# Sample rows of the input projection: four column groups hold quarters of the columns instead of parts of the contraction

## The reference

```python
D_MODEL, SEQ, DEC_BATCH, DEC_SEQ = 1024, 256, 8, 4
xn = rms_norm(x, p['norm_attn_g'])
z = jnp.einsum('btd,de->bte', xn, p['w_in'])
(qa, ck, cv, sk, sv, wk, wv, ng, fq, fk, fv, ff, ga, gb) = jnp.split(z, offs, axis=-1)
```

## Time and profile before

| | |
|---|---|
| median of 3 runs | 924.46 us |
| profiled execution, its own time | 927.73 us |
| its span | 926.0 us |
| TensorE busy | 858.2 us, 93% |
| VectorE busy | 513.4 us, 55% |
| ScalarE busy | 378.6 us, 41% |
| projection stage, first matmul to last ScalarE copy | 17.2 to 110.2 us |

### The profile page before, as it was taken

One profiled execution on the slowest core, in us unless ns is written; L12 is line 12 of the kernel. 1 busy time (PEld: TensorE's weight loads), 2 busy tenths in 40 slices (PEclk: granted clock), 3 DMA queues, 4 the chain that ended last, 5 costly groups with the idle time before them and its releaser, 6 DMA issues. The chain is left out here.

```text
span 926.0 us, 17951 instructions
## 1 busy us (share of the span) xinstructions
PE 858.2 (93%) x7159; PEld 703.4 (76%) x7159; DVE 513.4 (55%) x941; ACT 378.6 (41%) x704; POOL 161.3 (17%) x262
## 2 busy tenths in 40 slices
PE   4999878799999999999998977999979999999997
PEld 3788768689989977655754455997678998989985
DVE  5466567533434566754467434655656565565654
ACT  4346575633334324453224322444243443444432
POOL 2000041311121022333434510000001010110100
PEclk8999989999999899999999999999979999999999
DMA  6442096155424259999999995974054544555412
GB/s 219 150 160 105 10 316 236 60 145 134 165 107 184 92 229 398 346 333 416 406 417 420 388 404 169 297 250 164 10 196 142 162 137 136 177 195 171 136 45 61
DMA packets 90640, 191.89 MB, mean 207 GB/s; under 512 B 7466, under 2 KB 68682, under 8 KB 78186
## 3 DMA queue, kind: packets, MB, share of 16 engines
q0 software_dynamic: 15408, 106.04, 29.4%
q1 hardware_dynamic: 74876, 83.91, 29.0%
q10 hardware_dynamic: 288, 0.97, 0.3%
HBM read 187.44 MB, written 7.64 MB: 211 GB/s over the span
## 5 line engine op out<-in xcount | busy, mean ns | idle before, releaser
L1627 PEld LDWEIGHTS banks<-consts_base,stream_rows 128*128 128x128 f32 x672 | 73.2, 141 | 33.9 <-issue 26.8
L1875 ACT ACTIVATE keys_turned<-banks 128x512 f32<-128x512 f32 x94 | 55.0, 597 | 98.4 <-PE banks L1627 96.2
L258 PE MATMUL banks<-tokens_turned_high,w_gates_high 128*128 128x288 f32 x288 | 86.6, 301 | 3.3 <-PEq L191 2.3
L1627 PE MATMUL banks<-consts_base,stream_rows 128*128 128x128 f32 x672 | 82.7, 276 | 7.4 <-DVE fox_probs_turned L1866 2.6
L259 PE MATMUL banks<-tokens_turned_low,w_gates_high 128*128 128x288 f32 x288 | 85.5, 297 | 0.0
L1166 PE MATMUL banks<-chunks_turned_high,cmp_w_high 64*128 64x256 f32 (+1 forms) x512 | 78.6, 300 | 5.3 <-DVE cmp_w_low L251 2.7
L260 PE MATMUL banks<-tokens_turned_high,w_gates_low 128*128 128x288 f32 x272 | 81.8, 301 | 0.0
L1166 PE MATMUL banks<-chunks_turned_low,cmp_w_high 64*128 64x256 f32 (+1 forms) x512 | 75.4, 287 | 0.0
L1166 PE MATMUL banks<-chunks_turned_high,cmp_w_low 64*128 64x256 f32 (+1 forms) x512 | 75.1, 286 | 0.0
L1856 DVE COPY keys_turned<-banks 128x512 f32<-128x512 f32 x74 | 50.2, 689 | 32.7 <-PE banks L1627 30.2
L251 DVE TENSOR_TENSOR chunks_turned_low<-banks,chunks_turned_high 128x512 fp32r<-128x512 f32 x64 | 41.1, 683 | 46.9 <-ACT chunks_turned_high L246 46.9
(11 more groups left out here) (451 smaller groups left out, 2099.1 us busy)
## 6 DMA issues: line engine op xcount, KB each, us to landing
w_up_gate<-in_w_up SPq DMA_DIRECT2D x12, 1024.0 KB, 7.3
w_up_gate<-in_w_gate SPq DMA_DIRECT2D x12, 1024.0 KB, 9.8
w_down<-in_w_down SPq DMA_DIRECT2D x12, 1024.0 KB, 4.9
w_in_slot<-in_w_in SPq DMA_DIRECT2D x7, 1424.0 KB, 6.0
w_gates<-in_w_in SPq DMA_DIRECT2D x10, 512.0 KB, 6.8
cmp_w<-in_cmp_w_k SPq DMA_DIRECT2D x4, 512.0 KB
cmp_w<-in_cmp_w_v SPq DMA_DIRECT2D x4, 512.0 KB
stream_rows<-in_state_win_k SPq DMA_DIRECT2D x8, 256.0 KB
```

Of the source, the lines that this page charges most:

```text
L258: nc.tensor.matmul(out, lh, rh, start=start, stop=False, **kw)
L1627: ins = nc.tensor.transpose(bank(t)[:, q * P:(q + 1) * P], src, ident)
L1875: copy = lambda a, b: nc.scalar.activation(a, b, ACT.Copy)
```

## The change

`ZQ` = 89 is a quarter of a chunk's columns. Each column group now takes its own quarter of the columns and sums all 8 contraction steps, so the finished sample rows stand in the bank, each quarter at its own partitions. A contraction step is four matmuls of 89 columns with the same stationary rows. The folding product, the buffers `part` and the copy into them go. VectorE copies the four 32 x 89 pieces straight into `z`, at the place where `sample_part` stood. Counts of semaphores are adjusted: `z_out[0]` counts one a chunk, and `sample_out` takes the place of `fold_out`.

```diff
@@ constants
+ZQ = ZC // 4
@@ TensorE, for each chunk
                 if n >= 2:
-                    pe.wait_ge(z_out[0], 2 * n - 2)
+                    pe.wait_ge(z_out[0], n - 1)
                     pe.wait_ge(z_out[1], n - 1)
-                    pe.wait_ge(fold_out, n - 1)
+                    pe.wait_ge(sample_out, n - 1)
...
                 for k in range(KD):
-                    g = k % 4
                     if n == 0 and k % 4 == 0:
                         pe.wait_ge(w_first[k // 4], 16)
-                    m = nc.tensor.matmul(U[3 * u + 2][32 * g:32 * g + 32, 0:ZC], c.xsT[:, k, :], w[u][:, k, :], start=(k < 4), stop=(k >= 4))
+                    for g in range(4):
+                        m = nc.tensor.matmul(U[3 * u + 2][NS * g:NS * g + NS, 0:ZQ], c.xsT[:, k, :], w[u][:, k, g * ZQ:(g + 1) * ZQ],
+                                             start=(k == 0), stop=(k == KD - 1))
                 m.then_inc(z_sums, 1)
...
                 tokens(n, 0)
-                pe.wait_ge(z_out[0], 2 * n + 1)
-                nc.tensor.matmul(U[3 * u + 2][0:NS, 0:ZC], c.k("fold"), part[u], start=True, stop=True).then_inc(folded, 1)
...
@@ VectorE
-            def sample_part(n):
+            def sample_rows(n):
                 dve.wait_ge(z_sums, 3 * n + 1)
-                if n >= 2:
-                    dve.wait_ge(folded, n - 1)
-                nc.vector.tensor_copy(part[n % 2], U[3 * (n % 2) + 2][:, 0:ZC]).then_inc(z_out[0], 1)
+                if n == 0:
+                    dve.wait_ge(zeroed, 1)
+                for g in range(4):
+                    ins = nc.vector.tensor_copy(z[0:NS, 2, at(n) + g * ZQ:at(n) + (g + 1) * ZQ], U[3 * (n % 2) + 2][NS * g:NS * g + NS, 0:ZQ])
+                ins.then_inc(sample_out, 1)
...
-            def sample_rows(n):
-                dve.wait_ge(folded, n + 1)
-                if n == 0:
-                    dve.wait_ge(zeroed, 1)
-                nc.vector.tensor_copy(z[0:NS, 2, cols_of(n)], U[3 * (n % 2) + 2][0:NS, 0:ZC]).then_inc(fold_out, 1)
...
             for n in range(NZC):
-                sample_part(n)
+                sample_rows(n)
...
                 rows0(n)
-                sample_rows(n)
```

More of the change, by code:

```diff
@@ L383, in stage_project @@
         flat = c.h_rows[:, :, :].rearrange("p t d -> p (t d)")
-        part = [flat[:, u * ZC:(u + 1) * ZC] for u in range(2)]
         sq = flat[:, D:D + 3 * FW].rearrange("p (t h e) -> p t h e", t=3, e=HD)
@@ L393, in stage_project @@
         z_out = [c.sem(f"z_copied_{e}") for e in "va"]
-        z_sums, folded, fold_out, zeroed = c.sem("z_sums_ready"), c.sem("z_folded"), c.sem("z_fold_copied"), c.sem("z_sample_zeroed")
+        z_sums, sample_out, zeroed = c.sem("z_sums_ready"), c.sem("z_sample_copied"), c.sem("z_sample_zeroed")
         gains_in, gain_ready, zeros = c.sem("gains_in"), c.sem("q_gains_scaled"), c.sem("q_zeroed")
@@ L446, in turn @@
                 if bank == 0:
-                    pe.wait_ge(z_out[0], 2 * NZC - 2)
+                    pe.wait_ge(z_out[0], NZC - 1)
                 elif number[x] > 2:
@@ L461, in turn_tails @@
                 ins.then_inc(heads_turned, 1)
-                pe.wait_ge(fold_out, NZC - 1)
+                pe.wait_ge(sample_out, NZC - 1)
                 pe.wait_ge(chunks.pe_in, 32)
@@ L469, in turn_nsa_keys @@
                 pe.wait_ge(heads_ready, rank["KK"] + 1)
-                pe.wait_ge(z_out[0], 2 * NZC)
+                pe.wait_ge(z_out[0], NZC)
                 for t in range(3):
                     if t == 2:
-                        pe.wait_ge(fold_out, NZC)
+                        pe.wait_ge(sample_out, NZC)
                     bank = U[3] if t < 2 else U[5]
@@ L551, in square @@
                 n = complete[group]
-                act.wait_ge(z_out[0], 2 * n + 2)
+                act.wait_ge(z_out[0], n + 1)
                 act.wait_ge(z_out[1], n + 1)
-                act.wait_ge(fold_out, n + 1)
+                act.wait_ge(sample_out, n + 1)
                 if rank[group]:
@@ L677, in scale @@
                 dve.wait_ge(roots, rank[group] + 1)
-                dve.wait_ge(z_out[0], 2 * n + 2)
+                dve.wait_ge(z_out[0], n + 1)
                 dve.wait_ge(z_out[1], n + 1)
-                dve.wait_ge(fold_out, n + 1)
+                dve.wait_ge(sample_out, n + 1)
                 lo, heads = rs_at[group], sum(heads for _, heads in groups[group])
@@ L704, in forget_parts @@
                 ff = z[:, :, O_FF:O_FF + NH]
-                dve.wait_ge(z_out[0], 2 * NZC)
+                dve.wait_ge(z_out[0], NZC)
                 dve.wait_ge(z_out[1], NZC)
-                dve.wait_ge(fold_out, NZC)
+                dve.wait_ge(sample_out, NZC)
                 link(nc.vector.tensor_tensor(ff, ff, bcast(c.forget_bias[:, :], 1, 3), ALU.add))
```

## The result

The changed kernel takes 919.65 us (median of 8 runs, 917.43 to 923.14), the kernel before in the same number of runs 925.39 us (921.75 to 929.25). The two medians lie 5.7 us apart. The ratio is 0.9945 with a 95% interval of 0.992 to 0.997, which stands for 5.1 us saved, with an interval of 2.8 to 7.4. The forecast was 921.5 us and 3.0 us saved. Ratios and intervals here leave out one execution, of the run without folds in chunks 2 to 7, which took 1208 us at a mean granted clock of 0.66.

The account below looks back on a forecast made before the run. TensorE, 93% busy, was taken to bound the kernel. Folds -4.9, sample products +0.4 and the clock's fall +1.5 sum to -3.0 us, from the median 924.46 to 921.5 us, range 918.9 to 924.6.

Parts of the forecast that it names:

- The fixed point: Chunk 2's prompt tile starts at 44.04 us, set by its late load; TensorE time saved before it only lengthens the pause.
- The folds: Projection, chunks 2 to 7: removing six folding products of 0.81 us each saves 4.9 us; those of chunks 0 and 1 give nothing.
- The sample products: Chunks 3 to 7: 64 records of 89 columns cost 0.08 us more a chunk, 0.4 us in all, high end 2.7.
- the two-column row: Profile row of 29 two-column records, 22 ns each, giving 1.40 us for the sample part, 0.15 more a chunk.
- The clock: Chunk 2: after a pause grown to 3.05 us the clock falls to half, costing 1.5 us; forecast case chance 0.50.
- seven falls in eight pauses: Whole trace before: of eight pauses from 2.29 to 3.98 us begun at full clock, the clock fell after seven.
- The clock does not fall: Rival at chunk 2: full clock is kept after the longer pause, time 920.0 us; chance 0.26.
- A floor per record: Rival in the sample products: narrow records held by a minimum time each, 22 ns for two columns, time 923.8 us; chance 0.10.
- The saving is lost later: Rival in later stages: decoding's DMA or newly placed half-clock pauses take the saving back, 924.5 to 926 us; chance 0.09.
- Serial groups: Rival in chunks 3 to 7: column groups do not overlap, sample products take 4.9 us a chunk, time 939.5 us; chance 0.05.

Follow-up runs that it names:

- one group after the other: Changed kernel with all eight steps of one column group's sample products issued before the next group's, instead of in turn: 940.16 us in one profiled execution.
- the half width: Changed kernel with each sample product cut in two of 45 and 44 columns, groups still in turn: 918.96 us in one profiled execution.
- both moves: Chunk 2's load put ahead of the page numbers, small loads behind chunk 3's load: changed kernel 917.78 us, ratio 0.9916; kernel before 924.56 us, ratio 0.9997.
- the two fold runs: Kernel before with the folding product left out in chunks 0 and 1 only, ratio 1.003, or in chunks 2 to 7 only, ratio 0.995.
- the filled pause: Changed kernel with 16 unread matmuls of 288 columns added behind chunk 2's sample products: 917.31 us, ratio 0.9929.
- the load ahead: Changed kernel with chunk 2's load moved on SyncE's queue ahead of the gains and forget bias, behind the page numbers: 922.94 us, ratio 0.9974.

## Why the prediction was right, and where its sizes were off

**The fixed point** held. Chunk 2's tile starts between 43.67 and 44.76 us in the kernels whose loads were not moved (one group after the other aside), whenever TensorE comes, and leaving out the two folds ahead of it gains nothing. Its cause was told half: not the load's place on SyncE's queue alone, but also its slow transfer behind the tiny ones of the page numbers.

**The folds** were sized from the step between neighbouring starts, 0.81 us. The matmul behind the fold also holds the array 0.11 us longer where a prompt tile follows directly, in chunks 2, 3 and 4: 0.3 us that the sum lacked. In chunk 2 of the kernel before it is 48.84 to 49.12, where a step is 0.16:

```profile
49.12 0.32 PE L259 MATMUL banks<-w_in_low,tokens_turned_high 128*128 128x356 f32 x1
```

With it, 5.2 us were expected of the run that leaves these folds out, and 5.31 measured.

**The sample products** cost 0.03 us a chunk (1.36 against 1.34), 0.1 to 0.2 in all, not 0.4. The term that was mis-sized took its 0.08 us a chunk from the two-column row, whose order is another one. In proportion to the columns, 16 x 0.077 us, was right to 2%.

**The clock** fell at chunk 2 in the changed kernel's profile, from 45.5 to 48.9 us, and in that of the half width after a pause of 3.65 us. The price is 1.5 us, as forecast. The reason for the fall was told too simply. The prediction counted falls after pauses, and the length of a pause does not settle it. In the changed kernel the clock fell after one of 1.96 us:

```profile
485.53 3.42 PE L1621 MATMUL banks<-consts_base,stream_rows 128*128 128x128 f32 x16 [1.96 <-DMA stream_rows<-in_state_win_k]
...
485.90:489.20 3.30, 3.30 (x19) 2.86 (x21) 1.06 (x2) 1.40 (x3) 0.00 (x0) 0.50 1.01 420
```

After the pause of 2.94 us at the start of the next stage it stayed at 1.00 in five of the ten profiles until another pause had come. One is the changed kernel with both moves (104.51 us above):

```profile
104.50:109.40 4.90, 1.58 (x12) 1.39 (x12) 2.80 (x11) 4.83 (x8) 2.35 (x7) 1.00 0.73 146
```

And in the kernel before it fell once, at 300.5 us, with no pause over 0.3 us in the 10 us ahead, while TensorE was in 32 matmul records of 16 columns:

```profile
298.15 4.73 PE L1216 MATMUL banks<-cmp_k_turned,nsa_q_prompt 128*128 128x16 f32 x32
...
300.50:307.30 6.80, 6.80 (x54) 6.76 (x55) 0.00 (x0) 0.00 (x0) 0.00 (x0) 0.50 0.00 0
```

So seven falls in eight pauses made the fall look surer than it was. The chances of 0.50 with it and 0.26 without it were nearer the mark, and that it came in the profiled execution is in part luck.

Together from chunk 2's start: -4.9 - 0.3 + 0.15 + 1.5 = -3.55 us, measured -3.55. The forecast's -3.0 is off by 0.3 in the folds and 0.25 in the sample products.

**The rest of the 5.1 us** is not from the change as far as the runs show. In the profiled pair chunk 2 starts 0.7 us later, so the stage brings 2.8 us, and from the next stage's first matmul to the end of the span it is 812.8 us before and 809.9 after. These 2.9 us come about between instructions that are the same in both kernels. Before:

```profile
183.74 0.40 PE L1166 MATMUL banks<-chunks_turned_high,cmp_w_high 64*128 64x274 f32 x2 [2.71 <-DVE cmp_w_low L251]
...
338.17 1.94 PE L1627 MATMUL banks<-consts_base,stream_rows 128*128 128x128 f32 x16 [1.66 <-PEq L191]
```

After:

```profile
179.93 0.40 PE L1160 MATMUL banks<-chunks_turned_high,cmp_w_high 64*128 64x274 f32 x2 [2.71 <-DVE cmp_w_low L252]
...
329.75 1.94 PE L1621 MATMUL banks<-consts_base,stream_rows 128*128 128x128 f32 x16 [1.66 <-PEq L192]
...
532.68 0.27 PE L1767 MATMUL banks<-sample_rows_kept,nsa_probs_turned 128*32 128x128 f32 x1 [1.76 <-DMA stream_rows<-in_cache_sel_v,eighth_row]
```

The first stretch takes 154.4 us before, with 10.2 us at half clock in it, and 149.8 after, with none: 4.6 us less. The next, to the row at 538.91 us before and 532.68 after, takes 200.7 and 202.9 us: 2.2 more, with three falls of the clock in it that the kernel before did not have (424.4, 485.9 and 499.5 us). What stands ahead of and behind these stretches adds 0.5. The code there is the same. In the ten profiles of this case the last part of the program, from the next stage's start on, takes 807.3 to 812.8 us, in no order that follows the edits: 811.2 and 811.7 in the two fold runs, 811.4 with the filled pause, 812.5 with the load ahead, 807.3 at half the width. A single execution thus carries several us of chance, and the interval of the ratio, 2.8 to 7.4 us, holds the 3.5 us of the stage. Whether a systematic part remains between 3.5 and 5.1 is open. The mechanism of the forecast is worth 3.5 us; what the 5.1 measured have above that was not forecast, and no run ties it to the change.

**The rivals.** "The clock does not fall" is contradicted by the one profile of the changed kernel; how often it fell in the other executions is not known. A floor per record of 22 ns or more across the groups is refuted. "The saving is lost later" is not seen in the total, though the stretches of half clock that it spoke of did move: 2.2 us were lost in decoding and more was gained ahead of it. Serial groups do not happen in turn; written one after the other the sample products take 4.2 us a chunk, near the 4.9 that the prediction priced.

## What to carry to other kernels

Narrow matmuls that share the array by column groups keep their streaming time when cut along the columns, if the groups are issued in turn; then a product that only adds partial sums is pure cost, its two changes of array shape included. Work removed ahead of a late transfer turns into pause, and the clock of the work behind a longer pause may fall, so look for the last fixed arrival before counting instructions. To judge half a per cent, read the distance between two fixed events of the stage beside the total.

## What the runs showed of the hardware

- Forty-four columns in plain fp32 per record and four column groups in turn give one start each 10 ns; 89 columns give one each 19 ns (64 in 1.43 us, the last lasting 0.24).
- The same 64 records, one group after another, take 4.2 us: a group's first record starts before the previous group's last three and not earlier.
- At chunk 2 the clock fell after pauses of 2.13, 3.35 and 3.65 us and not after 1.37, 1.46, 1.51 and 1.97. Elsewhere it also fell after 1.92 and 1.96 us (changed kernel, 424.4 and 485.9 us) and stayed up after 2.29 and 2.94 us. Once it fell without such a pause, in matmuls of 16 columns (kernel before, 300.5 us).
- The folding product stands between matmuls of 128 output rows and has 32 itself. Its two changes of array shape lengthen the step ahead of it by 0.10 us and the one behind it by 0.12 (47.87 to 48.13 and 48.84 to 49.12, where a step is 0.16).
- A load of 1424 KB took 10.6 us from issue to first use behind the eight tiny loads of page numbers and the gains, 12.9 when issued directly behind the page numbers, and at most 7.0 ahead of them.
